# FFN block sums by accumulating transfers instead of GpSimd, in a two-layer streaming encoder

## The reference

```python
def conv_ffn(h, prev, w_gate, w_up, conv_w, conv_b, w_down):
    g = h @ w_gate                     # 1024 -> 2816
    gp = jnp.concatenate([prev.astype(g.dtype), g], axis=1)
    c = conv_b
    for j in range(CONV_W):            # 3 taps along the tokens
        c = c + conv_w[j] * gp[:, j:j + t]
    y = (jax.nn.gelu(c) * (h @ w_up)) @ w_down
```

## Time and profile before

| | |
|---|---|
| median of three runs | 2109.64 us |
| the profiled execution | 2105.28 us |
| its span, first to last instruction | 2103.5 us |
| TensorE, VectorE, ScalarE, GpSimd busy | 95%, 63%, 40%, 26% |
| mean granted clock of TensorE | 0.984 of full speed |
| FFN of layer 0 | about 580 to 1090 us of the span |
| FFN of layer 1 | about 1590 to 2100 us |

### The profile page before, as it was taken

One profiled execution on the slowest core, in us unless ns is written; L12 is line 12 of the kernel. 1 busy time (PEld: TensorE's weight loads), 2 busy tenths in 40 slices (PEclk: granted clock), 3 DMA queues, 4 the chain that ended last, 5 costly groups with the idle time before them and its releaser, 6 DMA issues.

```text
span 2103.5 us, 30087 instructions
## 1 busy us (share of the span) xinstructions
PE 1992.7 (95%) x11870; PEld 1731.5 (82%) x11870; DVE 1334.4 (63%) x1994; ACT 834.0 (40%) x1368; POOL 548.6 (26%) x594
## 2 busy tenths in 40 slices
PE   9999989999988899999899999999998979999988
PEld 7889668987778788989789888798776868988986
DVE  5452764344488778778754377643547977878783
ACT  4222643344354334233344346243534423433442
POOL 3012121001144433435210134100013443433431
PEclk9999999999989899999999999999999989999999
DMA  5324152246603123122221221624561312222221
GB/s 184 110 95 133 46 181 106 91 170 232 212 1 100 41 81 114 47 81 80 91 88 49 81 85 44 232 91 150 203 222 40 101 41 80 81 80 81 80 91 54
DMA packets 111067, 219.39 MB, mean 104 GB/s; under 512 B 7011, under 2 KB 52367, under 8 KB 110862
## 3 DMA queue, kind: packets, MB, share of 16 engines
q1 hardware_dynamic: 91234, 148.00, 20.7%
q0 software_dynamic: 19696, 69.47, 9.6%
HBM read 200.51 MB, written 18.24 MB: 104 GB/s over the span
## 4 chain that ended last, share of the span: by engine, by line
PE 66%; DVE 21%; issue 4%; DMA 4%; ACT 3%; POOL 1%; SPq 0%; DVEq 0%; ACTq 0%; POOLq 0%
PE bank L909 16%; PE bank L911 15%; PE bank L910 15%; DVE w_lo L2339 6%; DVE cv L2849 4%; DMA raw<-w_ffn_down 2%; DMA raw<-w_ffn_up 2%; PE bank L973 2%; PE bank L975 2%; PE bank L977 2%; DVE w_lo L2343 1%; DVE af L2861 1%; PE bank L1355 1%; PE bank L1371 1%; DVE xn L2369 1%
## 5 line engine op out<-in xcount | busy, mean ns | idle before, releaser
L2343 DVE TENSOR_TENSOR w_lo<-raw,w_hi 128x1024 fp32r<-128x1024 f32 x177 | 212.7, 1217 | 210.5 <-ACT w_hi L1724 207.0
L909 PE MATMUL bank<-w_hi,hT_lo 128*128 128x512 f32 x720 | 289.9, 403 | 1.2 <-DVE hT_lo L2395 0.7
L911 PE MATMUL bank<-w_hi,hT_hi 128*128 128x512 f32 x720 | 281.3, 391 | 0.0
L910 PE MATMUL bank<-w_lo,hT_hi 128*128 128x512 f32 x720 | 280.8, 390 | 0.0
L909 PE MATMUL bank<-hT_hi,w_lo 128*128 128x320 f32 (+2 forms) x800 | 254.5, 318 | 21.7 <-DVE hT_lo L2791 8.5
L911 PE MATMUL bank<-hT_hi,w_hi 128*128 128x320 f32 (+2 forms) x800 | 251.6, 314 | 0.0
L910 PE MATMUL bank<-hT_lo,w_hi 128*128 128x320 f32 (+2 forms) x800 | 251.5, 314 | 0.0
L1721 ACT ACTIVATE w_hi<-raw 128x1024 fp32r<-128x1024 f32 x132 | 138.5, 1055 | 276.2 <-PE bank L911 131.6
L1724 ACT ACTIVATE w_hi<-raw 128x1024 fp32r<-128x1024 f32 x177 | 182.6, 1051 | 130.8 <-PE bank L911 65.5
L2339 DVE TENSOR_TENSOR w_lo<-raw,w_hi 128x1024 fp32r<-128x1024 f32 x132 | 197.5, 1501 | 52.2 <-ACT w_hi L1721 51.7
L2409 DVE TENSOR_TENSOR x<-x,bank 128x512 f32<-128x512 f32 x160 | 109.6, 685 | 127.0 <-PE bank L911 125.5
(11 more groups left out here) (431 smaller groups left out, 4287.3 us busy)
## 6 DMA issues: line engine op xcount, KB each, us to landing
raw<-w_ffn_gate SPq DMA_DIRECT2D x44, 512.0 KB, 4.0
raw<-w_ffn_up SPq DMA_DIRECT2D x44, 512.0 KB, 5.1
raw<-w_ffn_down SPq DMA_DIRECT2D x22, 1024.0 KB, 4.8
kcX<-cache_mem_k POOLq DMA_DIRECT2D x16, 1024.0 KB, 6.3
vcX<-cache_mem_v POOLq DMA_DIRECT2D x16, 1024.0 KB, 6.9
raw<-w_in_even SPq DMA_DIRECT2D x13, 1024.0 KB, 5.3
raw<-w_in_odd SPq DMA_DIRECT2D x12, 1024.0 KB, 5.2
raw<-w_cq SPq DMA_DIRECT2D x8, 1024.0 KB, 7.4
```

The lines of the kernel that those rows point to most:

```text
L909: pe.matmul(out, wl, xh, start=first, stop=False)
L910: pe.matmul(out, wh, xl, start=False, stop=False)
L911: return pe.matmul(out, wh, xh, start=False, stop=last)
L2343: dve.tensor_tensor(w_lo[:, s, 0:n], raw[:, q % 2, UNIT * i:UNIT * i + n], flat(w_hi[:, s, 0:n]), ALU.subtract).then_inc(*lo_made.mark(c, u))
```

## The change

`weight_sum` issues transfers on GpSimd's queue in place of its additions. A new part "base" loads W01 from HBM into the buffer of S1; S1 adds W11 from HBM to it (`accum_op=ALU.add`); S3 adds W00 from HBM to W01 in `raw`; each of these is two transfers of 256 KB, for gate and for up. S2 adds the buffer of S1 to W00 in `raw`, and S4 adds that to W10, each one transfer of 512 KB from SBUF to SBUF. All sums are now plus signs; VectorE's result additions turn into subtractions where the sign needs it. "base" of unit j + 2 is issued at the end of step j. The copy `corner` of ScalarE and the addition `first_corner` of GpSimd are replaced by one VectorE addition each, `c11`, ahead of the split of A22. `t3F` and `n4F` are made by VectorE after `low_ts(1)`. In the first down group the refill of the next unit's S1 moves behind the unit's last steps: on ScalarE behind `high_a`, on VectorE behind all but the last additions of the group.

```diff
                 def weight_sum(j, part):
 
                     c = ("gu", l, j)
-                    q0, q1 = LOAD_OF[(c, 0)][0], LOAD_OF[(c, 2)][0]
+                    q0 = LOAD_OF[(c, 0)][0]
                     s1 = sum_at[1 if j else 0][:, :, :]
-                    if part == "S1":
-                        pool.wait_ge(*w_in[q0 % 2].at(q0))
-                        pool.wait_ge(*w_in[q1 % 2].at(q1))
+                    if part == "base":
                         if j == 1:
                             pool.wait_ge(*xn_made.at(f"ffn{l}", T - 1))
-                        out, a, b, op = s1, quarter(c, 0, 1), quarter(c, 1, 1), ALU.add
+                        elif j > 1:
+                            pool.wait_ge(*lo_made.at(("gu", l, j - 1), PARTS.index("S1")))
+                    elif part == "S1":
+                        pool.wait_ge(*sum_in["base"].at(l, j))
                     elif part == "S3":
-                        out, a, b, op = quarter(c, 0, 1), quarter(c, 0, 0), quarter(c, 0, 1), ALU.subtract
+                        pool.wait_ge(*w_in[q0 % 2].at(q0))
                     elif part == "S2":
                         pool.wait_ge(*lo_made.at(c, PARTS.index("A11")))
-                        pool.wait_ge(*pool_done.at("sum", l, j, "S3"))
-                        out, a, b, op = quarter(c, 0, 0), s1, quarter(c, 0, 0), ALU.subtract
+                        pool.wait_ge(*sum_in["S1"].at(l, j))
+                        pool.dma_start(quarter(c, 0, 0), s1, accum_op=ALU.add).then_inc(*sum_in["S2"].mark(l, j))
+                        return
                     else:
                         pool.wait_ge(*lo_made.at(c, PARTS.index("A12")))
-                        pool.wait_ge(*pool_done.at("sum", l, j, "S2"))
-                        out, a, b, op = quarter(c, 1, 0), quarter(c, 1, 0), quarter(c, 0, 0), ALU.subtract
-                    pool.tensor_tensor(out, a, b, op).then_inc(*pool_done.mark("sum", l, j, part))
+                        pool.wait_ge(*sum_in["S2"].at(l, j))
+                        pool.dma_start(quarter(c, 1, 0), quarter(c, 0, 0), accum_op=ALU.add).then_inc(*sum_in["S4"].mark(l, j))
+                        return
+                    out = quarter(c, 0, 1) if part == "S3" else s1
+                    k, e = {"base": (0, 1), "S1": (1, 1), "S3": (0, 0)}[part]
+                    for m, w in enumerate((io["w_ffn_gate"], io["w_ffn_up"])):
+                        src = w[l][4 * P * k:4 * P * (k + 1), 256 * j + P * e:256 * j + P * (e + 1)].rearrange("(k p) n -> p k n", p=P)
+                        dst = out.rearrange("p (k m) n -> p k m n", m=2)[:, :, m, :]
+                        mark = sum_in[part].mark(l, j) if m else sum_in[part].mark(l, j, m)
+                        if part == "base":
+                            pool.dma_start(dst, src).then_inc(*mark)
+                        else:
+                            pool.dma_start(dst, src, accum_op=ALU.add).then_inc(*mark)
 
                 def halo(f):

...
@@ -783,26 +790,21 @@
                     pool.tensor_copy(tailc[:, f, 0:2], g[:, SEQ:SEQ + HALO]).then_inc(*pool_done.mark("tail_p", l, f))
                     pool.tensor_copy(tailc[:, f, 2:2 + 2 * NB].rearrange("p (b w) -> p b w", b=NB), seqs[:, :, TS:TS + HALO]).then_inc(*pool_done.mark("tail", l, f))
 
+                weight_sum(0, "base")
                 norm_rstd(f"ffn{l}", [0])
+                weight_sum(0, "S1")
                 norm_rstd(f"ffn{l}", [1])
-                weight_sum(0, "S1")
+                weight_sum(0, "S3")
                 norm_rstd(f"ffn{l}", [2])
-                weight_sum(0, "S3")
-                norm_rstd(f"ffn{l}", [3])
                 weight_sum(0, "S2")
-                norm_rstd(f"ffn{l}", [T - 1])
+                norm_rstd(f"ffn{l}", [3, T - 1])
                 weight_sum(0, "S4")
-                pool.wait_ge(*act_done.at("hF", l, T - 1, 1))
-                pool.tensor_tensor(t3F[:, :, :], hF[:, 1, :, HT:TOK], hF[:, 0, :, HT:TOK], ALU.subtract).then_inc(*pool_done.mark("t3F", l))
-                pool.wait_ge(*dve_done.at("t2F", l, 1))
-                pool.tensor_tensor(hF[:, 1, :, 0:HT], hF[:, 1, :, 0:HT], t2F[:, :, :], ALU.subtract).then_inc(*pool_done.mark("n4F", l))
+                weight_sum(1, "base")
                 pool.wait_ge(*act_done.at("prevT", l))
                 for j in range(FT // 2):
                     more = j + 1 < FT // 2
                     halo(2 * j)
                     halo(2 * j + 1)
-                    first_corner(j, "g")
-                    first_corner(j, "u")
                     if more:
                         weight_sum(j + 1, "S1")
                         weight_sum(j + 1, "S3")
@@ -812,6 +814,8 @@
                     tails(2 * j + 1)
                     if more:
                         weight_sum(j + 1, "S4")
+                    if j + 2 < FT // 2:
+                        weight_sum(j + 2, "base")
                 pool.wait_ge(*act_done.at("rows", l))
                 pool.dma_start(io["o_conv_p"][2 * l:2 * l + 2, :], rows18[0:2, :]).then_inc(*put["rows"].mark(l, "p"))
                 pool.dma_start(io["o_conv_s"][2 * NB * l:2 * NB * (l + 1), :], rows18[2:2 + 2 * NB, :]).then_inc(*put["rows"].mark(l, "s"))
...
@@ -1704,7 +1708,7 @@
                         continue
                     part = PARTS[u] if c[0] == "gu" else ""
                     if part.startswith("S"):
-                        act.wait_ge(*pool_done.at("sum", c[1], c[2], part))
+                        act.wait_ge(*sum_in[part].at(c[1], c[2]))
                     else:
                         q, i = LOAD_OF[(c, {"A11": 0, "A12": 2, "A22": 2}.get(part, u))]
                         act.wait_ge(*(w_in[q % 2].at(q) if q or i else w_first.at(0)))
...
@@ -2133,10 +2128,13 @@
                     if kind == "dn":
                         if f is not None:
                             gelu(f)
-                            refill_hi(g0 + 4)
+                            if i:
+                                refill_hi(g0 + 4)
                             gelu(f + 1)
                             high_a(f)
                             high_a(f + 1)
+                            if i == 0:
+                                refill_hi(g0 + 4)
                         elif i < GROUPS - 1:
                             refill_hi(g0 + 4)
...
@@ -2154,16 +2152,14 @@
                         first_product(i, "u")
                     if f is not None:
                         high_a(f)
-                    corner(i, "g")
                     refill_hi(g0 + 5)
                     if f is not None:
                         high_a(f + 1)
-                    corner(i, "u")
                     if i == 0:
-                        high_t("t3", t3[0][:, :, :], t3F[:, :, :], 0, pool_done.at("t3F", l))
+                        high_t("t3", t3[0][:, :, :], t3F[:, :, :], 0, dve_done.at("t3F", l))
                     refill_hi(g0 + 6)
                     if i == 0:
-                        high_t("n4", n4[0][:, :, :], hF[:, 1, :, 0:HT], 0, pool_done.at("n4F", l))
+                        high_t("n4", n4[0][:, :, :], hF[:, 1, :, 0:HT], 0, dve_done.at("n4F", l))
                     refill_hi(g0 + 7)
                     refill_hi(g0 + 8)
...
@@ -2753,7 +2749,7 @@
                         for n in range(2):
                             if g < GROUPS - 1:
                                 if t == T - 1 and n == 0:
-                                    for k in range(1, units_of(c)):
+                                    for k in range(1 if g else 0, units_of(c)):
                                         refill_lo(FIRST_UNIT[c] + 4 + k)
                             elif behind and t == T - 1 and n == 1:
                                 split_lo(NEXT[c], [1, 2, 3])
...
@@ -2795,39 +2791,46 @@
                     low_t("t1", hT_hi[:, 0:4, w], hT_lo[:, 0:4, w], hF[:, 0, :, CUT[n]], n, n)
                     low_t("t2", t2[0][:, :, CUT[n]], t2[1][:, :, CUT[n]], t2F[:, :, CUT[n]], n, n)
 
+                def c11(j, key):
+
+                    c = ("gu", l, j)
+                    dve.wait_ge(*lin_a.at(c, (key, "A11")))
+                    dve.wait_ge(*lin_full.at(c, (key, "A12")))
+                    dst = gp[0][:, HALO:HALO + HT] if key == "g" else af[0][:, 0:HT]
+                    dve.tensor_tensor(dst, p1[key][:, :], lin.bank(c, (key, "A12"))[:, 0:HT], ALU.add).then_inc(*lin_v.mark(c, (key, "A12")))
+
                 def to_sums(j, key):
 
                     c = ("gu", l, j)
-                    dve.wait_ge(*pool_done.at("C11", l, j, key))
                     dve.wait_ge(*lin_full.at(c, (key, "S2")))
-                    dve.tensor_tensor(u2[key][:, :], p1[key][:, :], lin.bank(c, (key, "S2"))[:, 0:HT], ALU.add).then_inc(*lin_v.mark(c, (key, "S2")))
+                    dve.tensor_tensor(u2[key][:, :], lin.bank(c, (key, "S2"))[:, 0:HT], p1[key][:, :], ALU.subtract).then_inc(*lin_v.mark(c, (key, "S2")))
```

(32 more changed lines are left out.)

12 lines of the change are left out of this document (6 added, 6 removed).

## The result

Seven runs of the changed kernel took 2112.93 to 2117.74 us, median 2116.32. Seven of the kernel before, on the same chip, took 2107.26 to 2111.39, median 2109.07. The ratio is 1.0031 with a 95% interval of 1.0019 to 1.0042: slightly slower, where 2080 us and "faster" had been forecast. The time lies inside the range given.

What follows compares the result with a forecast made beforehand. TensorE, busy 95%, was taken as the bound, held up in the FFN by a blocked VectorE. Per layer 14 us gained, plus 3, minus 3 for traffic: 28 in both, so 2080 us predicted, range 2048 to 2142.

Steps and rivals of the forecast that it cites:

- What bounds the kernel, and the relief: FFN stages: TensorE waits for VectorE, which GpSimd's SBUF additions block; moving them to transfers shortens VectorE's forms, 3.29 to 1.28 us.
- Start, unit 1 and first down group: 14 us per layer: From layer start to the first down group's end: VectorE's shorter chain and the moved refill give 14 us per layer.
- some 8: First down group: TensorE's 11.6 us wait shrinks, and a wait of some 8 us stays.
- L = 6.5: Time from issue to landing of each 512 KB accumulation inside SBUF (S2, then S4): 6.5 us, bounds 4.5 and 9.8.
- The chain in unit 5: Odd unit 5: A12 split ends at 803.7, S2's split 813.7, `c11` 822.5; TensorE waits 2.9 us, against 2.5.
- half a microsecond on six tight loads is 3 us: Loads that start each unit: 1.5 MB more per unit from HBM costs 3 us per layer, bounds nothing and 6.
- likeliest case: The forecast itself: landing time of the SBUF accumulations 5.5 to 7.3 us, kernel 2060 to 2096 us, chance 0.45.
- ceiling: FFN of both layers: TensorE's listed waits, some 42 us per layer, cap any gain at 84 us.
- Late next: Odd units: VectorE waits for a transfer before S2's split; a microsecond of landing time costs 2 us per tight unit.
- The slower one: Odd units, S2's split: accumulation landing from 7.7 us becomes the bound; 2132 us at 8.5, 2170 at 9.8; chance 0.25.
- Not relieved: VectorE: preparing an accumulation holds SBUF as long as an addition did; near 2108 us; chance 0.10, with gains cancelled.
- fast landing: SBUF accumulations land in at most 5 us, tight units' waits under 1 us each: 2050 to 2060 us; chance 0.20.

Runs made afterwards that it cites:

- E10: The changed kernel with VectorE's part undone (`c11`, `t3F`, `n4F` back as before), transfers and moved refill kept: 2126.3 us.
- E12: The changed kernel with `c21` of up ahead of S2's split, S2 and S4 ahead of the tails copies, and both made by GpSimd additions: 2080.0 us.
- E4: The changed kernel with S1 and S3 accumulated for one row block of four only, three quarters of these sums left out: 2086.8 us.
- E11: The changed kernel with VectorE's and GpSimd's orders both changed, and S1 and S3 accumulated for one row block of four only: 2024.6 us.
- E2: The changed kernel with GpSimd's order alone changed, S2 and S4 each issued ahead of the tails copies: 2070.4 us.
- E13: The changed kernel with VectorE's and GpSimd's orders both changed, and S1's and S3's transfers writing instead of adding: 2046.0 us.
- E3: The changed kernel with both reorderings: `c21` of up ahead of S2's split, and S2 and S4 issued ahead of the tails copies: 2066.7 us.

## Why the prediction was wrong, by its own steps

*What bounds the kernel, and the relief.* Right. The gain products, the subtraction, L2849's form and the splits took the durations given. E10 and E12 confirm that VectorE's relief is worth time. That the excess was "about what a GpSimd addition lasts" holds for the start of the layer alone (2.0 and 2.7 us); in the earlier trace rows it is 1.0 to 1.2 us, and an addition lasted 2.4 to 3.4.

*Start, unit 1 and first down group: 14 us per layer.* Right. The first stretch shrank by 11.0 and 13.4 us; up to the end of the long wait it is 13.0 in layer 0 (682.15 - 579.78 against 693.89 - 578.52). The wait ended at 682 for "near 680". It lasts 5.4 us, and the forecast "some 8" doesn't follow from the prediction's own numbers: TensorE came to it at 693.89 - 11.64 = 682.25, 7 us earlier is 675.2, and up to 679.8 that is 4.6.

*L = 6.5.* Right for S2 (6.4), a microsecond short for S4 (7.5). At the prediction's own rate, 1 us per tight unit for a microsecond of S4, that is 5 us a layer that the sum lacked.

*The chain in unit 5.* Right in its links, wrong at its head. From the end of the A12 split to the end of S2's I had 803.7 to 813.7, 10.0 us; measured 797.3 to 807.7, 10.4. But the A12 split was to start 22.4 us after unit 4's high part (780.12, and its neighbours) and started 25.6 after it: S4's landing 1.3 us later than forecast, the load 2.3 us slower than before, 0.4 taken up. TensorE then waits 4.27 for `c21` and 1.72 for `c11`, 6.0 together for the 2.9 forecast.

*The step that failed:* "half a microsecond on six tight loads is 3 us". It was nearly five times that in unit 5 (2.3 us) and six times on average: 3.1 us over units 3, 5, 7, 9 and 10 (9.5 for 6.4). In units 5, 7, 9 and 10 the load and S4 together bring waits of 4.0 to 4.8 us for `af`, 17.8 us in all; net of the shorter waits that they replace they are most of the 12.1 us of idle time added in layer 0 (11.8 in layer 1). The term named bytes from HBM, 1.5 MB a unit, and no row for its half microsecond. I hadn't counted the packets of the accumulations, nor that SP's loads go through the same 16 DMA engines. The Trainium skill says this of the queues (DMA: Bandwidth & Descriptors, Issuing engines are not separate DMA queues): transfers started by any engine run on the same 16 and interleave. The trace agrees: 5.1 us became 7.4 on a queue of which nothing was changed. E4, with three quarters of S1's and S3's traffic gone, has those loads back at 6.6 us and takes away 30 of the 36 us between the forecast and the result; its 2086.8 lies inside the likeliest case's own 2060 to 2096.

*A term that was missing: the clock.* After each of the waits above 4 us the records show 3.4 to 6.8 us at half of the 2.4 GHz clock. That is the 6.7 us (6.1 in layer 1) by which the same 1547 matmuls were busy longer. Before, the waits for `p1g` there were 1.4 us at most and the granted clock was 1.00, so lengthening them to 4 cost more than the wait itself. The sum had no term for it. Nor had the "ceiling" of 84 us, which counted only TensorE's waits: E11 gains 84 with some 12 us of waits left in layer 0, and its TensorE is busy 1972.1 us and not the 1992.7 of the earlier trace rows, at a mean granted clock of 0.992 and not 0.984.

*Late next.* The place was named rightly ("VectorE, freed, stands before S2's split and waits for a transfer"), and so was the exchange: a microsecond on the chain is paid in each tight unit. What I took as given was GpSimd's order. The chain had "`c12` 0.6, GpSimd's tails 0.6" ahead of S2's accumulation, as program order has it; the sum's own conditions, A11's low part and S1's landing, were met by 793.1 in unit 5 (the low part ended at 793.07, S1's last transfer landed at 793.13), and it was issued at 798.99. E2 shows what these links are worth: 46 us.

*Rivals.* The slower one (decided by L above 7.7) was the right place by the wrong door: L stayed below, and the delay came through the loads. "Not relieved" is refuted, although its 2108 is nearest to the measured time; "fast landing" is refuted by 6.4 and 7.5 us.

*Open.* The split of the traffic's cost between bytes and additions rests on E11 and E13, which differ in bytes too; half and half is what they show, not more. No run changes the landing of the loads and nothing else. Whether fewer, longer pieces would accumulate cheaper wasn't tried.

## What to carry to other kernels

Moving additions from an engine into transfers frees what that engine was blocking, but a landing replaces a duration: 2.4 us of work became 6.4 to 7.5 us of latency. Issue such a transfer as soon as its own operands are there, ahead of anything in the queue that waits for something else; that order was worth 46 us here and 6 where the work was still done by an engine. And price added transfers by their packets as well as their bytes, on all loads with a deadline.

## What the runs showed of the hardware

An accumulating transfer goes in packets of one piece: 512 B in 65 ns (74 in E13, where all that are left are those inside SBUF), against 4096 B in 176 ns for the plain ones of E13's FFN. S3's two transfers of 256 KB, added from HBM, landed in 6.1 and 7.1 us in E3 and written, in E13, in 3.6 and 4.6. GpSimd's issue of an accumulating transfer lasts 1.3 to 1.9 us here, not the 0.9 of the earlier trace rows (the changed kernel, groups of GpSimd):

```profile
L760 POOL DMA_DIRECT2D raw<-sumN x20 | 33.5, 1677 | 10.7 <-DVE w_lo L2335 10.7
```

It cost nothing visible on VectorE, whose splits beside it kept their 1.22 us.
